# A hybrid decoder layer on one core: steps moved within a written-out order, and the last add and store cut in two

## The reference, cut to what matters

```
h = rms_norm(x);  proj = h @ w_in
u   = silu(layer_norm(causal_dwconv31(ca * sigmoid(cg))))        # group "conv", 512 channels
att = sparse_attention(qh, kh, vh, iq, ik, iw, rel_bias)         # group "att", 8 heads of 64
y   = rms_norm((ssd_scan(...) + d * xs) * silu(z))               # group "ssm", 8 heads of 64
x = x + concat([u, att, y]) @ w_out
h = rms_norm(x)
fa, fg = split(causal_dwconv3(h @ w_up))                         # 2 x 2816 columns
x = x + (silu(fg) * fa) @ w_down
```

## Time and profile before

| what | value |
|---|---|
| median of 3 runs | 709.29 us (709.13 to 709.3) |
| the profiled execution's own time | 709.14 us |
| its span in the profile | 707.4 us |
| PE busy | 691.9 us (98%) |
| DVE busy | 552.3 us (78%) |
| ACT busy | 374.6 us (53%) |
| POOL busy | 143.0 us (20%) |
| granted TensorE clock | full speed in all slices |

### The profile page before, as it was taken

How to read it: one execution, slowest core, us unless ns; L and a number is a source line. 1 busy time by engine, 2 the same in 40 slices (tenths; PEclk the granted TensorE clock), 3 DMA queues, 4 the chain that set the end, 5 groups by cost and what they waited for, 6 DMA issues and landing times.

```text
span 707.4 us, 9874 instructions
## 1 busy us (share of the span) xinstructions
PE 691.9 (98%) x3427; PEld 555.6 (79%) x3430; DVE 552.3 (78%) x866; ACT 374.6 (53%) x571; POOL 143.0 (20%) x126
## 2 busy tenths in 40 slices
PE   4999999999999999999999999999999999999998
PEld 4776888767777788788798888888888888888886
DVE  4468989999999967677668687786666775997995
ACT  6354555977888666544464434334344333654660
POOL 3000477945655305032400000000000000000000
PEclk9999999999999999999999999999999999999999
DMA  8641314212121251212336568856678647764442
GB/s 246 208 145 61 120 59 120 61 61 85 42 85 43 67 218 61 90 60 61 97 106 190 170 182 252 243 177 180 190 217 252 205 153 292 288 221 154 160 163 90
DMA packets 88443, 103.85 MB, mean 147 GB/s; under 512 B 6859, under 2 KB 67631, under 8 KB 88407
## 3 DMA queue, kind: packets, MB, share of 16 engines
q1 hardware_dynamic: 88263, 102.86, 46.1%
q10 hardware_dynamic: 144, 0.52, 0.2%
HBM read 86.84 MB, written 16.54 MB: 146 GB/s over the span
## 4 chain that ended last, share of the span: by engine, by line
PE 95%; ACT 2%; DMA 1%; POOL 1%; issue 1%; DVE 0%; ACTq 0%; DVEq 0%
PE bank L1799 82%; PE bank L1805 4%; PE bank L1985 2%; PE bank L1819 2%; PE bank L2009 2%; PE bank L1960 1%; DMA x_in<-in_x 1%; PE bank L1981 1%; PE bank L2075 1%; POOL stats L848 1%; PE bank L2084 0%; ACT u_tok L1167 0%; PE bank L2092 0%; ACT dec L1109 0%; ACT conv_hi L1172 0%
## 5 line engine op out<-in xcount | busy, mean ns | idle before, releaser
L1799 PE MATMUL bank<-h_hi,w_hi 128*128 128x512 f32 (+1 forms) x528 | 205.9, 390 | 0.0
L1799 PE MATMUL bank<-h_hi,w_lo 128*128 128x512 f32 (+1 forms) x528 | 202.4, 383 | 0.0
L1799 PE MATMUL bank<-h_lo,w_hi 128*128 128x512 f32 (+1 forms) x528 | 202.3, 383 | 0.0
L1799 PEld LDWEIGHTS bank<-h_hi,w_hi 128*128 128x128 f32 x528 | 99.3, 188 | 20.9 <-issue 2.3
L1799 PEld LDWEIGHTS bank<-h_hi,w_lo 128*128 128x128 f32 x528 | 99.2, 188 | 20.0
L1799 PEld LDWEIGHTS bank<-h_lo,w_hi 128*128 128x128 f32 x528 | 99.4, 188 | 18.2
L1653 DVE SCALAR_TENSOR_TENSOR f<-bank,prm,f 128x511 f32<-128x511 f32 x88 | 65.8, 747 | 60.4 <-ACT f L1199 54.9
L868 POOL TENSOR_TENSOR u_acc<-tapped,u_acc 128x511 f32<-128x511 f32 (+29 forms) x60 | 90.1, 1502 | 40.9 <-ACT tapped L1144 37.4
L1199 ACT ACTIVATE f<-bank,prm 128x512 f32<-128x512 f32 x44 | 34.2, 777 | 70.1 <-PE bank L1799 69.9
L648 DVE TENSOR_TENSOR w_lo<-w_raw,w_hi 128x2048 fp32r<-128x2048 f32 x24 | 55.9, 2328 | 5.0 <-ACT w_hi L944 4.9
L630 DVE SCALAR_TENSOR_TENSOR u_acc<-u_in,prm,u_acc 128x511 f32<-128x511 f32 (+29 forms) x60 | 54.3, 917 | 0.9
(11 more groups left out here) (280 smaller groups left out, 1197.0 us busy)
## 6 DMA issues: line engine op xcount, KB each, us to landing
w_raw<-in_w_up SPq DMA_DIRECT2D x44, 512.0 KB, 6.1
w_raw<-in_w_in SPq DMA_DIRECT2D x34, 512.0 KB, 4.6
down_raw<-in_w_down SPq DMA_DIRECT2D x22, 512.0 KB, 5.4
weight_sums<-down_raw SPq DMA_DIRECT2D x11, 768.0 KB, 5.3
w_raw<-in_w_out SPq DMA_DIRECT2D x12, 512.0 KB, 4.5
weight_sums<-w_sum SPq DMA_DIRECT2D x11, 512.0 KB, 2.7
w_raw<-weight_sums SPq DMA_DIRECT2D x6, 768.0 KB, 7.1
down_raw<-weight_sums SPq DMA_DIRECT2D x5, 768.0 KB, 5.8
```

Source lines behind the costliest of these rows:

```text
L1799: ins = pe.matmul(o, a, b, start=first and i == 0 and q == 0, stop=last and i == n - 1 and q == 2)
```

## The change

In `make_plan`, `attout` of blocks 1 and 2 is appended to the fill of its slot instead of its front; `lnT` and `clo` move one slot forward; and the low part of chunk 23, the first of the FFN (`UP0`), moves from slot 89 to the fill of slot 88, behind `("hi", 23)`. On PE the transposes `h2` of tile 1 leave their place in the list and are done between the two halves of the last `mg` step of the output product. At the end, the last add is done as two of 256 columns, each with a store of its own.

```diff
-LNT_SLOTS = (70, 70, 71, 71)
-CLO_SLOTS = (71, 71, 72, 72)
+LNT_SLOTS = (69, 69, 70, 70)
+CLO_SLOTS = (70, 70, 71, 71)
...
-        fill[4 * c - (2 if c == LATE_LO else 3)].append(("lo", c))
+        fill[4 * c - (2 if c == LATE_LO else 3 if c < UP0 else 4)].append(("lo", c))
...
-            front[n + 1].append(("attout", b))
+            (fill if b in (1, 2) else front)[n + 1].append(("attout", b))
...
-            for n, (t, half) in enumerate(((0, 1), (1, 1), (2, 1), (3, 1), (0, 0), (1, 0))):
+            for n, (t, half) in enumerate(((0, 1), (1, 1), (2, 1), (3, 1), (0, 0))):
                 sp.wait_ge(x_added, 14 + 4 + n + 1)
                 store(t, half)
-            sp.wait_ge(s_yout, 16 * 2 * NT)
+            for quarter in range(2):
+                f = slice(256 * quarter, 256 * quarter + 256)
+                sp.wait_ge(x_added, 14 + 4 + 5 + quarter + 1)
+                sp.dma_start(out[P:2 * P, f], x2[:, 1, f]).then_inc(s_yout, 16)
+            sp.wait_ge(s_yout, 16 * (2 * NT + 1))
...
-            for t in range(2):
-                dve.wait_ge(m_done, 12 + t + 1)
-                add_to(t, 0, bank[PAIR_BANK[2][t]][:, :], ALU.add)
+            dve.wait_ge(m_done, 12 + 1)
+            add_to(0, 0, bank[PAIR_BANK[2][0]][:, :], ALU.add)
+            dve.wait_ge(m_done, 12 + 2)
+            dve.wait_ge(x_added, added[(1, 0)])
+            for quarter in range(2):
+                c = slice(256 * quarter, 256 * quarter + 256)
+                dve.tensor_tensor(x2[:, 1, c], x2[:, 1, c], bank[PAIR_BANK[2][1]][:, c],
+                                  ALU.add).then_inc(x_added, 1)
...
                 elif k == "h2":
-                    turn_norm(x2n, "h2T", s[1])
+                    if s[1] != 1:
+                        turn_norm(x2n, "h2T", s[1])
...
+                    if (c, q) == (UP0 - 1, NT - 1):
+
+                        product(ps(*key)[:, :], terms[0:2], first=True, last=False)
+                        turn_norm(x2n, "h2T", 1)
+                        ins = product(ps(*key)[:, :], terms[2:4], first=False, last=True)
```

More of the change, by code:

```diff
@@ L1945, in _ @@
                     f = slice(P * q, P * q + P)
[L1946 to L1951, removed]
+                    terms = [(m_h[:, k0 + kk, f],
+                              conv_lo[:, q, kk, :] if m_l is conv_lo else m_l[:, k0 + kk, f],
+                              w_h[:, kk, :], w_l[:, kk, :]) for kk in range(4)]
+                    if (c, q) == (UP0 - 1, NT - 1):
+                        product(ps(*key)[:, :], terms[0:2], first=True, last=False)
+                        turn_norm(x2n, "h2T", 1)
+                        ins = product(ps(*key)[:, :], terms[2:4], first=False, last=True)
+                    else:
+                        ins = product(ps(*key)[:, :], terms, first=whole or i == 0,
+                                      last=whole or i == 1)
                     if whole or i == 1 or q == 3:
```

## The result

The changed kernel takes 712.88 us (median of 5 runs, 712.75 to 712.97), the kernel before, in turn with it, 709.29 (709.13 to 709.36). The ratio is 1.0052, 95% interval 1.0041 to 1.0062: slower, on the side that was forecast, 1.0 us beyond the predicted 711.9 and inside the range. The profiled execution took 712.97 us with a span of 711.2, 3.8 more than before.

A forecast was written before the change was run, and what follows sets the result against it. The prediction took PE, busy 691.9 of 707.4 us, to bound the kernel. It summed 709.14 + 3.7 - 0.56 - 0.55 + 0 = 711.73, plus 0.15 to the median: 711.9 us, range 709.9 to 713.6.

The forecast's parts named there:

- Part 1: `attout` of blocks 1 and 2 moved to the fill: DVE idles for `att_hi` behind `w_hi`; PE loses 3.7 us.
- All alone saves 1.4 us, five more slow ones cost 3.5: DVE's nine taps before the logits of unit 15: two slow beside POOL's adds before and after, so no difference.
- The 0.1 taken off as slack at `pv` 14: PE's `pv` of unit 14 starts 0.14 us after `evT` ends, counted as slack against DVE's 3.7 to 4.0 loss.
- Part 2: `lnT` and `clo` one slot earlier: +1.0 us stall at `lnT` 1, -1.56 us stall ahead of `dec`; -0.56 us.
- The lower bound of -1.56: Moved `lnT` and `clo`: the gain in us if `lnT` 1 did not wait.
- Part 3: Ahead of the FFN, early `w_lo` of chunk 23 and moved `h2` of tile 1: -0.55 us, bounds 0 and -1.36.
- the -0.69 for `up0`: PE starts `up0` at 357.7 instead of 358.39 us because `h_lo` of tile 1 ends earlier.
- the 0.15 held back for the last tile's `x2n`: Ahead of the FFN, the last tile's `x2n` follows the same DVE chain and costs 0.15 us of the gain.
- Part 4: Final add and store in two: DMA queue already full, so 0 us, between -0.3 and +0.3.
- The hidden wait: Rival: DVE or ACT makes up the 3.7 us before `pv` of unit 14; 708.2 us, chance 0.12.
- the half absorbed debt: Rival: taps no longer meet POOL's adds and block 1's gain counts fully, leaving 1.9 us; 710.1 us, chance 0.10.
- New stalls without their return: Rival: `lnT` 1 waits 1.0 us but `dec` comes no earlier; 713.5 us, chance 0.14.

The follow-up runs named there:

- e1: The changed kernel with `attout` of block 2 back in the front of its slot; 708.43 us, ratio 0.9986.
- e2: The kernel before with only `attout` of block 2 moved to the fill; 714.18 us, ratio 1.0070.
- e12: The changed kernel with POOL's additions of taps 24 to 29 of channel quarter 2 cut to 8 columns; 710.46 us, ratio 1.0016.
- e13: The kernel before with POOL's additions of taps 24 to 29 of channel quarter 2 cut to 8 columns; 709.11 us, ratio 1.0002.
- e5: The kernel before with only `lnT` and `clo` one slot earlier, as in the change; 708.69 us, ratio 0.9988.
- e6: The kernel before with `lnT` and `clo` one slot earlier, except `lnT` 1 and `clo` 1; 708.58 us, ratio 0.9985.
- e11: The kernel before with `lnT` at slots 69, 70, 70, 71, `clo` at 70, 71, 71, 72, and `w_lo` of chunk 23 early; 707.89 us, ratio 0.9980.
- e9: The kernel before with only `w_lo` of chunk 23 moved to slot 88; 708.93 us, ratio 0.9991.
- e8: The kernel before with only the `h2` transposes of tile 1 moved inside the last `mg` step; 709.27 us, ratio 0.9997.
- e10: The kernel before with only the final addition and last store in two parts; 709.25 us, ratio 1.0002.
- e3: The changed kernel with `attout` of blocks 1 and 2 at the head of the fill, ahead of `("hi", 15)`; 711.36 us, ratio 1.0030.
- e4: The changed kernel with `attout` of blocks 1 and 2 in a fourth list read behind `fill`, last in the slot; 709.93 us, ratio 1.0009.

## Why the prediction was right, and where it was short

**Part 1, the wait.** Right in place and in kind: `att_hi` behind `w_hi`, DVE idle, the waits of PE for `prob` and `probT`, and e1 and e2 show by removing and adding the one move that the loss is its own. The debt behind the wait was forecast at 3.7 us and measured 3.65. That DVE's idle time is 4.79 and not 3.7 to 4.0 costs nothing: DVE reached the wait earlier, and ACT's `w_hi` sets its end. That the 3.65 is so close has some luck in it: the sum took 0.38 off because DVE's logits would come 0.38 earlier, and they came 1.22 earlier; what ACT gained, 0.40, was set by its own `evT` (e2).

**Part 1, the size.** The step that failed is "All alone saves 1.4 us, five more slow ones cost 3.5 ... so I take no difference". The term was +1.0: the taps took 0.85 us more and `w_lo`, of which the sum had not thought, 0.69 more, and the later taps gave back 0.55. The pair e12 and e13 shows all of it to be the meeting with POOL, since without POOL's additions the debt does not grow (3.64 to 3.56). The 1.4 that all taps alone would save was right (1.44 in e13), but in the changed kernel they were not alone. The 0.1 taken off as slack at `pv` 14 was wrong too: the distance from `evT`'s end to PE's start is 0.14 in both kernels (246.40 to 246.54 after), a hand-over. So the term of 3.7 measured 4.6.

**Part 2.** Right: -0.56 forecast, -0.57 measured in the changed kernel and in e5, with both halves (+1.0, -1.6) where they were put. That the whole stall went was a near thing: `dec` came 0.61 earlier and not the 1.1 of the working, and in e5 its last exp ends at 290.79, while the PE instruction that needs it starts at 290.98, when its turn has come. The lower bound of -1.56 was not reached by any order that was run (e6, e11).

**Part 3.** The power at 0.55 us, the missing wait for `x2n` and the 0.4 us of the chain were right. The 0.55 was too much: the -0.69 for `up0` counted nearly all of the 0.37 between `h_lo` and PE as slack; the 0.15 held back for the last tile's `x2n` did not come and hid half of that. The term measured -0.39, and e9 has -0.37 by the early `w_lo` alone, e8 nothing by the split.

**Part 4.** Right: nothing, within 0.1 (e10).

**The rivals.** The hidden wait and the half absorbed debt fell: the debt came out larger and not smaller, and the meeting with POOL, from which the second took its gain, went the other way. New stalls without their return fell with e5. With 4.60 for 3.7, -0.57 for -0.56, -0.39 for -0.55 and 0.11 for 0, the sum is 709.14 + 3.75 = 712.89; the profiled execution took 712.97; of the rest, 0.03 is start-up. So the 1.0 beyond the forecast is nearly all the taps and `w_lo` of part 1.

**The lower clock** cost PE time without costing the kernel any: it lay between two waits for DVE and ACT, and 0.72 us of waiting were left behind it. It is the main reason why PE's two named waits come to 2.6 us and not the 3.7 that the prediction looked for. The chain that `pv` 14 waits for does not pass through the slow matmuls: DVE has no idle time from 222.93 to the logits of unit 15 at 240.62, and ACT's exps start on these logits and go on without a gap to `evT`. e3 and e4 kept the full clock, and PE's delay was DVE's debt there as well. A kernel at full clock that has the whole 4.64 of debt was not run.

## What to carry to other kernels

When a step moves within its slot, ask on each engine what the other half of the step stands behind: here one `append` put a 0.6 us copy behind a 1.9 us one on ScalarE, and VectorE, which had no idle time before, stood for 4.8 us. A debt on a full engine isn't constant on its way to TensorE: it moves every later instruction against GpSimd's work, and that added a quarter to it here. And take a gap between a releaser's end and TensorE's start as hand-over, not as slack, until another instance of it is shorter.

## What the runs showed of the hardware that was not expected

- TensorE's granted clock was 0.50 (1.2 GHz) from 229 to 232 us, right behind a wait of 1.90 us ahead of which it had run the short products `score` and `pv`; matmuls of 512 columns then started 0.43 us apart instead of 0.23. It was 0.95 from 232 to 233. After a wait of 2.28 us in e2, behind the same products, it was 0.60 from 228.2 to 229 and 0.54 from 229 to 232. After a wait of 1.06 us in e12, behind the same products, and after one of 1.68 us in e3, behind twelve `mg` matmuls, it stayed at 1.00.
- The low part of a weight chunk, a VectorE operation with both inputs in SBUF, takes 3.04 us beside POOL's additions (changed kernel) and 2.28 with these cut short (e12). Four taps take 3.75 and 2.91.
- Where it waits for them, TensorE starts 0.36 us behind the end of VectorE's `h_lo` (e8) and 0.14 behind the end of ScalarE's `evT` (changed kernel).
